# Attention scores three units ahead, four probability blocks, and another order of the sparse layer's projections

## What is computed

```python
def nsa_mixer(x, ...):                       # layer 0
    q, kc, vc, ks, vs, kw, vw, gl = jnp.split(x @ w_in, cuts, axis=-1)
    q_rot = apply_rope(q, cos, sin)
    k_slc, v_slc = apply_rope(kv_heads(ks), cos, sin), kv_heads(vs)
    k_win, v_win = apply_rope(kv_heads(kw), cos, sin), kv_heads(vw)
    k_cmp = compress(kv_heads(kc), ...)
    v_cmp = compress(kv_heads(vc), ...)
    # per head and query: softmax over compressed keys (q), selected and window keys (q_rot)
    return gc[..., 0:1] * o_c + gc[..., 1:2] * o_s + gc[..., 2:3] * o_w   # then @ w_o
def fox_mixer(x, w_in, b_f, w_o):            # layer 1
    q, k, v, fl = jnp.split(x @ w_in, [HQ, 2 * HQ, 3 * HQ], axis=-1)
    cum = jnp.cumsum(jax.nn.log_sigmoid(fl + b_f), axis=-1)
    logits = q k^T * scale + cum[:, :, s0:s1, None] - cum[:, :, None, :s1]
    # causal softmax, times v, @ w_o
x = layer_norm(ALPHA * x + y);  x = layer_norm(ALPHA * x + conv_ffn(x))
```

## Time and profile before

| | us |
|---|---|
| median of 3 runs | 1389.68 (1387.82 to 1391.71) |
| profiled execution | 1391.82, its span 1390.0 |
| TensorE busy | 1332.6 (96%) |
| VectorE busy | 666.7 (48%) |
| ScalarE busy | 656.1 (47%) |
| GpSimd busy | 604.5 (43%) |
| layer 0, units 0 to 127 | about 92 to 330 of the span |
| layer 1, units 128 to 191 | about 777 to 972 of the span |

### The profile page before, as it was taken

One profiled execution on the slowest core, in us unless ns is written; L12 is line 12 of the kernel. 1 busy time (PEld: TensorE's weight loads), 2 busy tenths in 40 slices (PEclk: granted clock), 3 DMA queues, 4 the chain that ended last, 5 costly groups with the idle time before them and its releaser, 6 DMA issues.

```text
span 1390.0 us, 19809 instructions
## 1 busy us (share of the span) xinstructions
PE 1332.6 (96%) x6858; PEld 1110.8 (80%) x6858; DVE 666.7 (48%) x1471; ACT 656.1 (47%) x1225; POOL 604.5 (43%) x398
## 2 busy tenths in 40 slices
PE   8979999989999999999999899998999999999997
PEld 6868887767888888888888788787788888888886
DVE  3347777774744334330017766768364433341006
ACT  4347677775344444441113767767244444443120
POOL 2267777653434444445434222222245444444441
PEclk9999999999999999999999999999999999999999
DMA  9442322223223333324232321222423333334321
GB/s 298 101 104 57 89 70 71 71 67 121 79 79 101 102 94 99 97 91 136 93 90 93 85 62 48 79 69 69 152 75 109 104 91 92 104 93 134 97 69 61
DMA packets 172798, 131.98 MB, mean 95 GB/s; under 512 B 24544, under 2 KB 156244, under 8 KB 172724
## 3 DMA queue, kind: packets, MB, share of 16 engines
q1 hardware_dynamic: 172724, 131.02, 32.3%
HBM read 117.17 MB, written 4.39 MB: 87 GB/s over the span
## 4 chain that ended last, share of the span: by engine, by line
PE 78%; DVE 10%; issue 4%; ACT 2%; DMA 2%; POOL 2%; SPq 2%; DVEq 0%; POOLq 0%; ACTq 0%
PE ps L955 15%; PE ps L956 15%; PE ps L957 15%; PE ps L1209 7%; PE ps L1212 7%; PE ps L1210 7%; PE ps L1115 2%; DVE xt L1639 2%; PE ps L1129 2%; PE ps L1082 2%; DVE ptl L1501 1%; DVE prob L1483 1%; SPq L343 1%; DVE xt L1629 1%; DVE stats L1633 1%
## 5 line engine op out<-in xcount | busy, mean ns | idle before, releaser
L487 POOL TENSOR_TENSOR wl<-raw,wh 128x1024 fp32r<-128x1024 f32 x178 | 432.5, 2433 | 659.0 <-ACT wh L609 658.9
L955 PE MATMUL ps<-xh,wh 128*128 128x512 f32 x968 | 382.8, 395 | 0.0
L957 PE MATMUL ps<-xh,wl 128*128 128x512 f32 x968 | 378.3, 391 | 0.0
L956 PE MATMUL ps<-xl,wh 128*128 128x512 f32 x968 | 378.2, 391 | 0.0
L609 ACT ACTIVATE wh<-raw 128x1024 fp32r<-128x1024 f32 x192 | 201.6, 1051 | 197.8 <-PE ps L1212 189.9
L957 PEld LDWEIGHTS ps<-xh,wl 128*128 128x128 f32 x968 | 182.2, 188 | 39.5
L955 PEld LDWEIGHTS ps<-xh,wh 128*128 128x128 f32 x968 | 182.5, 188 | 35.6 <-ACT qf L683 1.2
L956 PEld LDWEIGHTS ps<-xl,wh 128*128 128x128 f32 x968 | 182.5, 189 | 33.6
L1660 DVE SCALAR_TENSOR_TENSOR work<-ps,conv,work 128x511 f32<-128x511 f32 x88 | 65.9, 749 | 222.0 <-ACT work L838 156.2
L703 ACT ACTIVATE prob<-prob,negmax 128x128 f32<-128x128 f32 x192 | 107.4, 559 | 69.9 <-DVE negmax L1483 68.0
L1209 PE MATMUL ps<-wh,gh 128*128 128x512 f32 x352 | 139.1, 395 | 0.0
(11 more groups left out here) (196 smaller groups left out, 1968.5 us busy)
## 6 DMA issues: line engine op xcount, KB each, us to landing
raw<-in_ffn_w_up SPq DMA_DIRECT2D x88, 512.0 KB, 3.8
raw<-in_ffn_w_down SPq DMA_DIRECT2D x44, 512.0 KB, 3.5
raw<-in_fox_w_in SPq DMA_DIRECT2D x24, 512.0 KB, 4.0
raw<-in_nsa_w_in SPq DMA_DIRECT2D x12, 512.0 KB, 5.1
xt<-in_x SPq DMA_DIRECT2D x8, 512.0 KB, 5.1
raw<-in_nsa_w_in SPq DMA_DIRECT2D x16, 256.0 KB, 3.7
qs<-work SPq DMA_DIRECT2D x32, 128.0 KB, 2.3
raw<-in_nsa_w_o SPq DMA_DIRECT2D x8, 512.0 KB, 3.8
```

The source lines that it names most:

```text
L487: nc.gpsimd.tensor_tensor(wl[:, slot, :, :], raw[:, slot, :, :], wh[:, slot, :, :].bitcast(F32), ALU.subtract).then_inc(s_wl, 1)
L955: nc.tensor.matmul(o, ah, bh, start=start, stop=False)
L956: nc.tensor.matmul(o, ah, bl, start=False, stop=False)
L957: return nc.tensor.matmul(o, al, bh, start=False, stop=stop)
```

## The change

It does the following:
- Scores run three units ahead of the turn, as do maximum and exponential; `prob` has a fourth block (`prob3`, in layer 1 `fprob3`), chosen by `prob_at`. There are still two banks for scores, so scores of u+3 wait for the maximum of u+1.
- The items of a group come in the order keys, queries 0, values, queries 1 (`KIND`), with the waits and counts that follow from it. The extra piece of VectorE for the values is in iteration 3 of its block, `values_turn` in unit 25 of a group instead of 19.
- `qf` has one block instead of two, whose copy waits for the compressed scores that read it (that makes room for `prob3`).
- Lead-in of layer 0: item 1 (now queries 0) is projected before the hidden products; the compressed scores' mask and maximum come before the values' low part; the last item's steps are split around `values_turn`.
- Layer 1: the first turn of a pair stands behind the pair's first four projection steps instead of before them. In the lead-in the logarithm stands before the queries' copies and the scan before the queries' low part; the sign of the stored rows is made by a fill with -1 on the other operand instead of two negations.

The core of the diff (the rest are counts, declarations and the same shift on other lines):

```diff
+KIND = (0, 2, 1, 3)
+        def prob_at(u, n):
+            if u % 4 < 3:
+                return prob[:, u % 4, 0:n]
+            return (prob3 if u < NSA_UNITS else fprob3)[:, 0:n]
...
             def item_copy(g, k):
-                n = 4 * g + k
+                n, k = 4 * g + k, KIND[k]
                 act.wait_ge(s_wu, 4 + n + 1)
                 if n and k < 2:
                     act.wait_ge(s_pl, n)
...
-                    for x in ([0, 1, 2] if u == 0 else [v + 2]):
+                    for x in ([0, 1, 2, 3] if u == 0 else [v + 3]):
...
-                    if u + 2 < NSA_UNITS:
-                        nsa_scores(u + 2)
+                    if u + 3 < NSA_UNITS:
+                        nsa_scores(u + 3)
...
-                    if v == 19 and g < GROUPS - 1:
+                    if v == 25 and g < GROUPS - 1:
                         pe.wait_ge(s_cl, u // 16 + 1)
                         values_turn(g + 1)
...
-                    if v + 2 < 8:
-                        fox_scores(U + v + 2, v + 2, par, pair, None)
+                    if v + 3 < 8:
+                        fox_scores(U + v + 3, v + 3, par, pair, None)
                     elif more:
-                        fox_scores(U + v + 2, v - 6, 1 - par, pair + 1, rows_next)
-                    if v == 0:
-                        turn(U + v, v % 4)
+                        fox_scores(U + v + 3, v - 5, 1 - par, pair + 1, rows_next)
...
                         fox_pv((U + v - 3) // 2)
-                    if v:
-                        turn(U + v, v % 4)
+                    turn(U + v, v % 4)
...
-                if u >= 3:
-                    dve.wait_ge(s_pt, u - 2)
+                if u >= 4:
+                    dve.wait_ge(s_pt, u - 3)
...
-                    if turned and w == (6 if item[1] == 1 else 1):
+                    if turned and w == (3 if item[1] == 2 else 1):
                         item_dve(*item)
```

More of the change, by code:

```diff
@@ L565, in _ @@
                     item = (g, 3) if v < 8 else (g + 1, v // 8 - 1)
-                    turned = (v < 8 or g < GROUPS - 1) and item[1] != 1
+                    turned = (v < 8 or g < GROUPS - 1) and item[1] != 2
                     if u + 1 < NSA_UNITS:
@@ L596, in _ @@
             for g in range(GROUPS):
-                for n in range(2):
+                for n in (0, 2):
                     RAW_EXTRA[(4 + 4 * g + n) % R] += 1
             def landed(c):
-                return sum(2 if 4 <= x < C_WO0 and (x - 4) % 4 < 2 else 1 for x in range(c + 1) if x % R == c % R)
+                return sum(2 if 4 <= x < C_WO0 and x % 2 == 0 else 1 for x in range(c + 1) if x % R == c % R)
             def hi(c, slot, n=None):
@@ L774, in _ @@
                         heads_hi(u // 16 - 1, oh)
-                    if turned and w == (3, 5, 2, 2)[item[1]]:
+                    if turned and w == (3, 2, 2, 2)[item[1]]:
                         item_hi(*item)
@@ L907, in fox_stages @@
                 for v in range(8):
[L908 to L909 removed]
+                    if more or v + 3 < 8:
+                        unit_exp(U + v + 3, (v + 3) % 4)
                     if more and v == 7:
@@ L1043, in values_turn, with item_steps @@
                 last.then_inc(s_px, 1)
-            def item_steps(n):
-                if n:
+            def item_steps(n, first=0, last=KB):
+                if n and not first:
                     pe.wait_ge(s_pf, n)
-                for kk in range(KB):
+                for kk in range(first, last):
                     kstep(4 + n, (4 + n) % R, kk)
-            pe.wait_ge(s_kc, 3)
-            item_steps(0)
-            conv_turn(0)
-            cmp_hidden(1)
-            pe.wait_ge(s_kc, 4)
-            item_steps(1)
-            pe.wait_ge(s_gel, 2)
-            for g in range(GROUPS):
-                for hb in range(2):
-                    last = nc.tensor.matmul(ps[0:NCMP, 4, g * HD:(g + 1) * HD], ghid[:, hb, g * NCMP:(g + 1) * NCMP], w2v[:, hb, :],
-                                            start=(hb == 0), stop=(hb == 1))
-            last.then_inc(s_cmpo, 1)
-            pe.wait_ge(s_pl, 1)
-            values_turn(0)
-            item_steps(2)
-            conv_turn(1)
             def nsa_scores(u):
@@ L1085, in bank_free @@
             def bank_free(H):
-                n = 4 * ((H + 1) // 4) + 2
-                if n < NSA_ITEMS:
+                n = 4 * ((H + 1) // 4) + 3
+                if H and n < NSA_ITEMS:
                     pe.wait_ge(s_pl, n)
@@ L1104, in cmp_turn @@
                 pe.wait_ge(s_cp, j + 1)
+                if not j:
+                    pe.wait_ge(s_pl, 3)
                 for i in range(QT):
@@ L1155, in first_tile @@
                 down_half(c0 + k, k, 0, h, oh, ol, OUT_AT, k == 0, False)
+            pe.wait_ge(s_kc, 3)
+            item_steps(0)
+            conv_turn(0)
+            item_steps(1)
+            cmp_hidden(1)
+            pe.wait_ge(s_kc, 4)
+            item_steps(2)
+            pe.wait_ge(s_gel, 2)
+            for g in range(GROUPS):
+                for hb in range(2):
+                    last = nc.tensor.matmul(ps[0:NCMP, 4, g * HD:(g + 1) * HD], ghid[:, hb, g * NCMP:(g + 1) * NCMP], w2v[:, hb, :],
+                                            start=(hb == 0), stop=(hb == 1))
+            last.then_inc(s_cmpo, 1)
             pe.wait_ge(s_cmpr, 1)
             cmp_scores(0)
-            item_steps(3)
+            conv_turn(1)
+            item_steps(3, 0, 4)
+            pe.wait_ge(s_cmask, 1)
+            values_turn(0)
+            item_steps(3, 4)
             pe.wait_ge(s_vc, 4)
@@ L1563, in _ @@
             last.then_inc(s_cmpr, 1)
+            cmp_mask(0)
+            cmp_difference(0)
+            conv_copy(1)
             item_dve(0, 2)
-            conv_copy(1)
-            for step in (cmp_mask, cmp_difference, cmp_sum, cmp_inverse, cmp_gate, cmp_scale):
+            for step in (cmp_sum, cmp_inverse, cmp_gate, cmp_scale):
                 step(0)
```

138 lines of the change are left out of this document (74 added, 64 removed).

## The result

The changed kernel takes **1393.75 us** (median of 12 runs, 1391.93 to 1395.34) against 1389.63 us (12 runs) of the kernel before on the same chip; the ratio is 1.0024, 95% interval 1.0013 to 1.0036. The forecast was 1375.2 us (1366 to 1385), a gain of 1%; the kernel became 0.24% slower. The two profiled executions differ less, 1392.0 against 1390.0 us of span; the ratio of the runs is what counts.

A forecast was written before the change was run, and what follows sets the result against it. The prediction took TensorE, busy 1332.6 of 1390.0 us, as the bound, with some 57 us to win. Gains of 2.8 + 3.1 + 5.0 + 0.5 + 2.1 + 1.0 = 14.5 us gave 1375.2 us, range 1366 to 1385.

The forecast's parts named there:

- Lead-in of the sparse layer: Start to the sparse layer's first turn: turn at 92.2 instead of 95.0, queries wait gone; gain 2.8 us (0 to 5.6).
- Groups 0 to 2: Sparse layer's first three groups: waits at first scores go, a unit more room helps; gain 3.1 us (0 to 8).
- Last group: Sparse layer's last group: VectorE's 6.1 us of waits for exponentials go; gain 5.0 us (1 to 9.1).
- Forgetting layer, lead-in: Before the forgetting layer's first turn: cumulated gates stored some 2.2 us earlier; gain 0.5 us (0 to 2.2).
- The seven pairs: Forgetting pairs with a next one: 1.1 us wait hidden, new 0.8 us keys wait; gain 2.1 us (0 to 7.7).
- Last pair: Last forgetting pair: one maximum done before it, one stall of the first turn covered; gain 1.0 us (0 to 2).
- The new wait does not show: Rival, forgetting pairs: keys reached 0.8 us earlier, so all 7.7 us are won; 1369.6 us, chance 0.14.
- The extra unit is worth little: Rival, sparse groups: in-order stalls and GpSimd's low parts set the pace, 1.9 of 8.1 us remain; 1381.4 us, chance 0.16.
- The collision before the keys: Rival, forgetting pairs: GpSimd's block split holds the scaling before the keys' low part, 13.3 us more; 1388.5 us, chance 0.07.
- The clock at the new waits: Rival, forgetting pairs: 0.8 us waits drop the granted clock to 0.50, losing 24 us; 1399 us, chance 0.05.
- 0.88 for a gain: Whole kernel: chance 0.88 of being faster by over 0.3% (4.2 us); the same 0.07, slower 0.05.

The follow-up runs named there:

- VectorE's alone: Changed kernel with, on VectorE in the sparse layer, the low part of unit u-1 ahead of the maximum of unit u+3: 1429.43 us, ratio 1.0273.
- ScalarE's swap: Changed kernel, sparse layer: high part of unit u ahead of exponential of u+3 on ScalarE, 1384.83 us; with two units ahead there (exponential of u+2), 1402.76 us.
- both together: Changed kernel, sparse layer: low part ahead of the maximum on VectorE and high part ahead of the exponential on ScalarE: 1384.21 us, ratio 0.9965.
- the copies first: Changed kernel, forgetting layer: ScalarE's values copy ahead of the exponential, keys' copies ahead of high part and maximum: 1383.77 us, ratio 0.9948.
- the two that add ScalarE's swap: Changed kernel with the copies first and ScalarE's swap: 1377.08 us; also with VectorE's low part ahead of the maximum in the last sparse group: 1374.04 us.

## Why the prediction was wrong, step by step

- **Lead-in of the sparse layer: right.** Turn 0 at 91.75 for 92.2, the 4.7 us wait gone. The chain is the one that was followed, each link within 1 us: the queries' low part ends at 79.9 (79.0), VectorE's copy of the compressed values at 83.8 (82.8), the values' low part at 87.8 (87.1), the scale at 89.5 (90.0); the late start and the quicker end make up for each other. The third maximum costs 0.9 us, of which the step had counted 0.5. It did not count that the kernel before went through its first scores at half clock.
- **Groups 0 to 2: the failed step, by its sign.** The waits at the groups' first scores went (1.9 us), and the new order of items wins 3.35 us with two units ahead (181.38 to 178.03), up to 0.8 of it the clock's, for a forecast of 3.1. That is luck: the forecast gave 1.2 us of its 3.1 to the third unit, as half of the waits for scaled probabilities. Those grew from 2.5 to 3.3 us, and the third unit costs 4.0. "The same place in the order" was read as the same time. I looked at which operation stands where on VectorE, and not at which width now stands there, nor at ScalarE's order at all.
- **Last group: the failed step, the largest.** The loop score, maximum, exponential, inverse was taken for the bound, since 6.1 us of waits hung on it and its sum of 1.5 us was near the pace of 1.65 (by the turns it is 1.67; the maximum, put at 0.56 us, has a mean of 0.48 in the earlier trace rows). All those waits went and nothing was won: 53.78 us for a forecast of 5.0 us less than 51.84, at the same loss by the clock. The wait that counted was TensorE's own for low parts, 7.1 us in the same stretch, which I had named in one half-sentence ("an exponential first") without a price. Two units ahead, high part behind exponential behind maximum behind score was already the chain.
- **Forgetting layer, lead-in: right** in kind (0.9 us for 0.5; bounds 0 to 2.2).
- **The seven pairs: the third failed step; two of three terms right.** The 1.1 us was hidden, and the new wait for the keys came and costs 0.76 us a pair for 0.8. Missed, so put at nothing, was what the old place of the turn had hidden: the first projection step now comes before it and stands 0.6 us on the copy of the values. 1.1 - 0.6 - 0.76 = -0.26 us, and a pair became 0.24 us longer. The count was wrong as well. Only six of the seven pairs had the 1.1 us wait; in the first of them the changed kernel waits 1.27 us for the keys at 789.35.
- **Last pair: wrong.** Six other kernels of this study with the same forgetting layer took 12.7 us for its last six units, as before (12.62). The 14.26 us of the changed kernel's profiled execution hold a stretch in which the clock fell; so 1.6 of the 2.0 us between the two profiles is of that execution and not of the change. The gain of 1.0 us did not come in any profile. The stall of the first turn was to be covered, but no projection steps stand before it in this pair (0.86 us at 954.58 for 1.10), and the products then wait 1.36 us for a low part where it was 0.82.
- **The rivals.** "The new wait does not show" fell: it shows, at 0.76 us a pair (0.5 of it listed as idle). "The extra unit is worth little" was nearest in mechanism (0.16, 1381.4), and it too had no loss in it. *The collision before the keys* did not come: the scaling of 128 columns at a pair's first unit is still held (1.87 us at 847.85, with GpSimd's split from 847.25 to 849.64), and now costs nothing, because the turn comes later (852.93, without a wait). The prediction's reading of the Trainium skill, "SBUF — State Buffer", section "Who interferes with whom", that the change covers this conflict and does not remove it, agrees with these rows. *The clock at the new waits* did not come either: twelve waits of 0.5 to 0.6 us in the pairs left it at 1.00. The Trainium skill, "TensorE: Matmul & The Clock Gate", section "HAM oscillation — how this bites in real kernels", tells of a kernel that fell back at every step, with waits of some 3 to 5 us each; waits as short as these are not its case.
- **The chances.** 0.88 for a gain rested on the waits taken away being worth something. No rival had a price for what stands behind the removed wait in the same queue, and the one that gave the sparse layer only 1.9 us still counted 2.1 us for the pairs.

## What to carry to other kernels

A deeper run-ahead on in-order engines does not only add slack: it changes which unit's work stands in front of the operation that the busy engine waits for, so write down the order of every engine in the chain, with widths, before giving it a price. Put what the bottleneck waits for ahead of what is merely early, and follow the swap through every engine of the chain. One swap can close a loop (VectorE's alone made the changed kernel 2.5% slower). Another, ScalarE's, won 0.6% with three units ahead, as much as both together, and lost 1.1% with two. When a move hides a wait, ask what the wait itself was hiding.

## What was not expected of the hardware

The granted clock fell to the 1.2 GHz level in the last pair of the changed kernel, in its profiled execution:

```profile
967.10:970.50 3.40, 3.40 (x15) 3.00 (x16) 2.20 (x6) 0.77 (x2) 0.00 (x0) 0.57 0.00 0
```

TensorE had just waited 1.36 us for a low part; in the last sparse group such a fall came 1.1 us behind the wait of 1.47 us shown above, and one as far behind another of 1.59 us. But waits of 1.33 and 1.41 us (at 324 and 330 us) had none behind them, and six profiles of the same forgetting program, with the same wait (1.36 or 1.37 us), showed no fall at that place. With the copies first, one profile has no fall there (12.71 us for the last pair) and the two that add ScalarE's swap have one (14.26 and 14.25). The wait alone does not decide it, and what does is open. A difference of one or two microseconds is no evidence for a cause here in a single profile with a fall in the stretch; the losses that this text puts on the third unit stand at the same clock. And a gain in a stage with many waits can be mostly the clock's, as the 3.3 us of ScalarE's swap in the last group.
